# Input and forget gate projection of a two-layer trunk: eight weight columns stationary and 512 tokens streamed, in place of token blocks stationary and eight columns streamed

## The chip, the cores and the metric

The kernel runs on one core of one Trainium2 chip. The metric is the device time of one execution in microseconds (us). Three runs of the kernel before took 2545.02, 2545.56 and 2546.22 us; their median, 2545.56 us, is the time it is compared by. Engines are called PE (TensorE), PEld (TensorE's weight loads), DVE (VectorE), ACT (ScalarE), POOL (GpSimd) and SP (SyncE, which issues the DMAs).

## What is computed

Two layers run over 512 tokens of width 1024. Each layer is a half-step feed-forward block, a token mixer and a second half-step feed-forward block, each followed by a layer norm. The mixer is fed by one projection, cut here to what matters:

```
proj = x @ w_in + b_in
(aq, ak, av, mq, mk, mv, mo, mi, mf, cx, cb, cc, gates) = jnp.split(proj, _split_points(), axis=-1)
...
h = mlstm_chunkwise(mq..., mk..., mv..., mi, mf)      # mi, mf: 4 columns each, one per head
...
fc = chunk3(jax.nn.log_sigmoid(f_pre.astype(f32)))    # in mlstm_chunkwise; ic is i_pre itself
b = jnp.cumsum(ft, axis=-1)
```

The change is about `mi` and `mf`, the input and forget gates of the four mLSTM heads: 8 of the 7432 columns of `w_in`.

## The kernel before

The stream `x` lies transposed in on-chip memory, as 8 blocks (`k`) of 128 features by 512 tokens. Every large product is made of three matmuls in fp32r, a reduced format that PE takes in one pass: high part of the weights by high part of the stream, low by high, and high by low (lines 1341, 1342 and 1345). ACT makes the high parts by a copy that rounds (`wh`, `xh`), DVE the low ones by a subtraction (`wl`, `xl`).

Weights come in slabs of up to 1024 by 256, two slots in turn. For each slab SP loads `raw`, ACT writes `wh`, DVE writes `wl`, and PE runs the slab's matmuls, 128 stationary weight columns against 512 streamed tokens each. A slab can have a "middle job", work that PE does when half of its features are through, and an "end job" behind it. Nothing plans the order: on each engine it is that of the code in `mixer`, slab by slab (s = 0 to 39), and semaphores join the engines.

The gates do not go through slabs. The 8 columns are loaded into `wif` as they are (line 481). Behind slab 0, `gate_products` (line 1424) makes 32 matmuls in full fp32, 4 token blocks by 8 feature blocks: 128 by 128 of `x` is stationary and the 8 columns of `wif` are streamed (line 1430). The result has the tokens on the partitions, 8 columns for each token block. In s = 0 DVE adds the bias (line 1036), and DVE and ACT work out the logarithm of the sigmoid by turns (lines 1036 to 1042 and 671 to 675). In slab 2 the middle job turns the result by two transposes (lines 1443 and 1444), and scans follow.

While slab 0 runs, the layer norm ends: ACT writes `xh` and the final `x` block by block (lines 588 and 582), DVE writes `xl` (line 966). `stat_sums` has matmuls whose result is not used, in `keep_clock`, between its small ones (line 1372).

Of the kernel before, what the change touches and what calls it, by code (L numbers as in the profile page):

```python
# [73 lines left out]
def build(nc, xT, positions, w_in, w_branch, w_out, gu1, down1, gu2, down2, par_in, const_in, outT):  # L74
    ctx = ExitStack()
    with ctx:
# [83 lines left out]
        rst = place("rst", [P, 4])  # L160
        mrow = place("mrow", [1, 96])
        wif = place("wif", [P, KD, 8])
        lut = place("lut", [P, 1])

        tok = place("tok", [P, 5, NB])
# [14 lines left out]

        positions_in = tmp("positions_in", 8, [P, SEQ], I32)
        turns = tmp("turns", 8, [P, SEQ])
        angle = tmp("angle", 10, [P, SEQ])
        rf, ri, rb, ra, rloc, rg, rm, rz = (tmp(f"row{i}", 0.5 * i, [16, P]) for i in range(8))

# [67 lines left out]

        raw_in = [[Signal(f"raw_in{s}{h}", 16 * (S_LAYER // 2 + 1)) for h in range(2)] for s in range(2)]
        wif_in = Signal("wif_in", 16)
        start_in = Signal("start_in", 0)
        x_in = [Signal(f"x_in{k}", 0) for k in range(4)]
        pos_in = Signal("pos_in", 16)
# [47 lines left out]
        f_exp = Signal("f_exp", 1)  # L306
        f_one = Signal("f_one", 1)
        f_ln = Signal("f_ln", 1)
        gates_tok = Signal("gates_tok", 1)
        gate_in = Signal("gate_in", 1)  # L310
        rows_ps = Signal("rows_ps", 1)
# [52 lines left out]
        def f32(a):  # L364
            return a.bitcast(F32)
# [154 lines left out]
        def _(act):  # L520
# [146 lines left out]
            def memory_gates(layer, s):  # L667

                if s == 0:
                    act.wait_ge(gate_in.sem, gate_in.val(layer, 1))  # L670
                    act.activation(gs[:, :], gf[:, :], ACT.Abs).then_inc(*o.up(f_abs))
                    o.settle()
                    act.activation(gs[:, :], gs[:, :], ACT.Exp, scale=-1.0).then_inc(*o.up(f_exp))
                    act.wait_ge(f_one.sem, f_one.val(layer, 1))
                    act.activation(gs[:, :], gs[:, :], ACT.Ln).then_inc(*o.up(f_ln))
                if s == 4:
                    act.wait_ge(decay_row.sem, decay_row.val(layer, 1))
                    act.activation(mrow[0:1, 80:96], mrow[0:1, 64:80], ACT.Exp).then_inc(*o.up())
                    act.wait_ge(g_rows.sem, g_rows.val(layer, 1))

                    act.activation(rf[:, :], rg[:, :], ACT.Exp, bias=rz[:, 0:1], scale=-1.0).then_inc(*o.up())
                    act.activation(ri[:, :], rm[:, :], ACT.Exp, scale=-1.0).then_inc(*o.up())
                    act.activation(rb[:, :], ra[:, :], ACT.Exp, bias=rz[:, 1:2]).then_inc(*o.up(exp_rows))
# [41 lines left out]
                act.activation(yMh[:, h, :], ytmp[:, :], ACT.Copy).then_inc(*o.up(ym_hi))  # L725

            def mixer(layer):
                for s in range(S_MIX):
                    n = S_FFN + s
                    if s == 0:  # L730
                        split_half(layer, n + 1, 1)
                    else:
                        split(layer, n + 1)
                    if 7 <= s < 15:
                        attn_out(layer, s - 7)
                    if s >= 18 and s < 30:
                        h, r = divmod(s - 18, 3)
                        if r == 0:
                            mem1(layer, h)
                        if r == 1:  # L740
                            mem3(layer, h)
                        if r == 2:
                            mem4(layer, h)
                    if s < 18:
                        evacuate(layer, s)
                    elif s < 36:
                        t, r = divmod(s - 18, 3)
                        if r < 2:
                            act.wait_ge(slab_done.sem, slab_done.val(layer, n + 1))
                            for m in range(2):  # L750
                                b = B_G + 8 * BRANCH_ORDER[t // 2] + 4 * (t % 2) + 2 * r + m
                                if t > 0:

                                    act.wait_ge(prod.sem, prod.val(layer, 4 * (t - 1) + 2 * r + m + 1))
                                act.activation(gt[:, 2 * r + m, :], pm[2 * r + m][:, :], ACT.Sigmoid,
                                               bias=par[:, b:b + 1]).then_inc(*o.up(sig_ready))
                        elif t >= 4:
                            for m in range(4):
                                k = 4 * (t - 4) + m
                                act.wait_ge(merged.sem, merged.val(layer, k + 1))  # L760
                                act.activation(mh[k // 4][:, k % 4, :], x[:, k, :], ACT.Copy).then_inc(*o.up(mg_hi))
                    if s in (0, 4):
                        memory_gates(layer, s)
                    if 6 <= s < 14:
                        attn_pT(layer, s - 6)
                    if 5 <= s < 13:
                        attn_exp(layer, s - 5)
                    if s in (15, 16):
                        for c in (2 * (s - 15), 2 * (s - 15) + 1):
                            act.wait_ge(yc_f.sem, yc_f.val(layer, c + 1))  # L770
                            act.activation(yCh[:, c, :], convtmp[:, :], ACT.Copy).then_inc(*o.up(yc_hi))
                    if s == 23:

                        act.wait_ge(slab_done.sem, slab_done.val(layer, n + 1))
                        for c in range(4):
                            act.activation(yAh[:, c, :], yA[:, c, :], ACT.Copy).then_inc(*o.up(ya_hi))
                    if s >= 18 and s < 30 and (s - 18) % 3 == 0:
                        mem2(layer, (s - 18) // 3)
                    if s == 37:
                        centre_copy(layer, 1)  # L780
                        squares(layer, 1, 0)
                        squares(layer, 1, 1)
                    if s in (37, 38):
                        squares(layer, 1, 2 * (s - 36))
                        squares(layer, 1, 2 * (s - 36) + 1)
                norm_tail(layer, 1, n + 2)
# [66 lines left out]
        def _(dve):  # L853
# [173 lines left out]
                o.settle()  # L1027

            def memory_gates(layer, s):
                if s == 0:  # L1030

                    dve.wait_ge(gate_ps.sem, gate_ps.val(layer, 1))
                    g = sd[:, 3, 0:32].rearrange("p (n g) -> p n g", g=8)
                    for dst, c in ((gi, 0), (gf, 4)):
                        bias = par[:, PAR_IF + c:PAR_IF + c + 4].unsqueeze(1).broadcast_to([P, NB, 4])
                        ins = V.tensor_tensor(dst[:, :].rearrange("p (n h) -> p n h", h=4), g[:, :, c:c + 4], bias, ALU.add)
                    ins.then_inc(*o.up(gate_in))

                    dve.wait_ge(f_exp.sem, f_exp.val(layer, 1))
                    V.tensor_scalar(gs[:, :], gs[:, :], 1.0, None, ALU.add).then_inc(*o.up(f_one))  # L1040
                    dve.wait_ge(f_ln.sem, f_ln.val(layer, 1))
                    V.scalar_tensor_tensor(out=gf[:, :], in0=gf[:, :], scalar=0.0, in1=gs[:, :],
                                           op0=ALU.min, op1=ALU.subtract).then_inc(*o.up(gates_tok))
# [193 lines left out]
                dve.wait_ge(proj.sem, proj.val(layer, proj_count(s)))  # L1237

            def mixer(layer):
                for s in range(S_MIX):  # L1240
                    n = S_FFN + s
                    if s == 0:
# [2 lines left out]
                        split(layer, n + 1)  # L1245
                    h, r = divmod(s - 18, 3)

                    if s in (2, 3, 4, 5):
                        memory_gates(layer, s)
                    if 18 <= s < 30:  # L1250
                        (mem1, mem3, mem4)[r](layer, h)

                    if s == 0:
                        memory_gates(layer, s)
                        dve.wait_ge(table_ready.sem, table_ready.val(layer, 1))
                    if s == 1:
                        rope(layer, 0, q[:, 0, :], 0)
# [51 lines left out]
        def _(pe):  # L1309
# [113 lines left out]

            def gate_products(layer):

                pe.wait_ge(wif_in.sem, wif_in.val(layer, 16))
                pe.wait_ge(norm_ready.sem, norm_ready.val(layer, KD))
                for n in range(NB):
                    for k in range(KD):
                        ins = T.matmul(sd[:, 3, 8 * n:8 * n + 8], x[:, k, P * n:P * n + P], wif[:, k, :],  # L1430
                                       start=k == 0, stop=k == KD - 1)
                ins.then_inc(gate_ps.sem, 1)

            def rotate(layer, r, t, bank, s):
# [3 lines left out]
                T.matmul(sd[:, bank, :], const[:, K_ROT:K_ROT + P], t, start=True, stop=True).then_inc(rot_ps.sem, 1)  # L1438

            def middle_job(layer, s):  # L1440
                if s == 2:
                    pe.wait_ge(gates_tok.sem, gates_tok.val(layer, 1))
                    T.transpose(sd[0:16, 2, 0:128], gf[:, :], ident)
                    T.transpose(sd[0:16, 2, 128:256], gi[:, :], ident).then_inc(rows_ps.sem, 1)
# [253 lines left out]
```

## Time and profile before

| | |
|---|---|
| median of three runs | 2545.56 us |
| the profiled execution, first to last instruction (span) | 2544.7 us |
| PE busy | 2515.7 us, 99% of the span |
| PEld busy | 2053.7 us, 81% |
| DVE busy | 1131.2 us, 44% |
| ACT busy | 973.2 us, 38% |
| POOL busy | 217.8 us, 9% |
| mean granted TensorE clock | 0.993 of full |
| main matmuls, each of the three kinds | 2336 on `xh` or `xl`, 704 on the hidden layer, and 320 more |

The profile gives no time of its own for that execution beside the span. Each matmul's recorded duration holds its way through the array, so that rows overlap (0.39 us long, but starting 0.23 us apart); what a stretch of matmuls costs is read from the distance of their starts. The fp32 matmuls of the gates stand in the trace as two records each.

### The profile page before, as it was taken

How to read it: one execution, taken by the hardware profiler on the slowest of the kernel's cores; microseconds unless marked ns; L12 is line 12 of the kernel's file. 1: busy time of each engine (PE TensorE's matmuls, PEld its weight loads, DVE VectorE, ACT ScalarE, POOL GpSimd, SP SyncE). 2: the span in 40 equal slices, each digit the busy share in tenths (PEclk: the TensorE clock that was granted, in tenths of full speed). 3: DMA queues.
4: the chain of work that ended last, by engine and by line, in shares of the span. 5: the costliest groups of instructions: out<-in, count | busy, mean ns of one | idle time of the engine just before them, and what ended most of it. 6: DMA issues, size and time to landing. Idle time of an engine off the chain costs nothing.

```text
span 2544.7 us, 31255 instructions
## 1 busy us (share of the span) xinstructions
PE 2515.7 (99%) x11378; PEld 2053.7 (81%) x11378; DVE 1131.2 (44%) x1584; ACT 973.2 (38%) x1334; POOL 217.8 (9%) x136
## 2 busy tenths in 40 slices
PE   8999999999999999999999999999999999999997
PEld 7888877778888778888788888787788887888886
DVE  3333344455555653333433333544455547433335
ACT  4443233344343354432344432424344433544323
POOL 0002120000000310001200021200000003000012
PEclk9999999999999999999999999989999999999999
DMA  5233232222222222322233323222222232332232
GB/s 166 90 98 99 92 88 75 77 73 83 83 83 83 96 81 89 97 95 92 95 100 99 97 92 101 55 92 67 83 83 83 68 98 83 99 99 89 90 107 79
DMA packets 229324, 229.05 MB, mean 90 GB/s; under 512 B 9440, under 2 KB 220640, under 8 KB 229216
## 3 DMA queue, kind: packets, MB, share of 16 engines
q1 hardware_dynamic: 229216, 227.66, 28.1%
q8 instruction: 62, 1.02, 0.2%
q14 instruction: 46, 0.38, 0.0%
HBM read 225.53 MB, written 2.10 MB: 89 GB/s over the span
## 4 chain that ended last, share of the span: by engine, by line
PE 95%; issue 2%; DVE 2%; POOL 1%; ACT 0%; DMA 0%; DVEq 0%; POOLq 0%; SPq 0%
PE main L1341 29%; PE main L1345 29%; PE main L1342 29%; PE side L1555 1%; PE side L1430 1%; DVE x L972 1%; DVE xl L966 1%; POOL ln_Q L838 1%; PE side L1377 1%; PE side L1507 1%; PE side L1541 0%; PE side L1392 0%; PE main L1372 0%; PE side L1565 0%; POOL ln_S L837 0%
## 5 line engine op out<-in xcount | busy, mean ns | idle before, releaser
L1341 PE MATMUL main<-xh,wh 128*128 128x512 f32 x2336 | 923.2, 395 | 8.7 <-ACT xh L550 7.3
L1345 PE MATMUL main<-xl,wh 128*128 128x512 f32 x2336 | 915.2, 392 | 2.1 <-DVE xl L966 1.2
L1342 PE MATMUL main<-xh,wl 128*128 128x512 f32 x2336 | 912.5, 391 | 0.0
L864 DVE TENSOR_TENSOR wl<-raw,wh 128x1024 fp32r<-128x1024 f32 (+1 forms) x443 | 538.9, 1250 | 626.6 <-ACT wh L541 619.8
L541 ACT ACTIVATE wh<-raw 128x1024 fp32r<-128x1024 f32 (+1 forms) x443 | 431.2, 1013 | 544.7 <-PE main L1345 537.1
L1341 PEld LDWEIGHTS main<-xh,wh 128*128 128x128 f32 x2336 | 440.4, 189 | 110.5 <-issue 12.2
L1345 PEld LDWEIGHTS main<-xl,wh 128*128 128x128 f32 x2336 | 440.0, 188 | 106.6 <-DVE xl L966 13.3
L1342 PEld LDWEIGHTS main<-xh,wl 128*128 128x128 f32 x2336 | 440.4, 189 | 91.3 <-issue 1.4
L1341 PE MATMUL main<-hh,wh 128*128 128x512 f32 x704 | 273.9, 389 | 0.0
L1342 PE MATMUL main<-hh,wl 128*128 128x512 f32 x704 | 273.9, 389 | 0.0
L1345 PE MATMUL main<-hl,wh 128*128 128x512 f32 x704 | 273.9, 389 | 0.0
L987 DVE SCALAR_TENSOR_TENSOR hp<-main,sil 128x512 f32<-128x512 f32 x88 | 56.7, 686 | 322.0 <-PE main L1345 322.0
L606 ACT ACTIVATE hh<-hp 128x512 f32 x88 | 54.4, 636 | 317.8 <-DVE hp L987 317.8
L1345 PEld LDWEIGHTS main<-hl,wh 128*128 128x128 f32 x704 | 132.2, 188 | 27.7
L1342 PEld LDWEIGHTS main<-hh,wl 128*128 128x128 f32 x704 | 132.2, 188 | 27.6
L1341 PEld LDWEIGHTS main<-hh,wh 128*128 128x128 f32 x704 | 132.2, 188 | 27.1
L831 POOL TENSOR_TENSOR ln_Z<-x 128x512 fp32r<-128x512 f32 x6 | 13.2, 2196 | 1555.1 <-DVE x L889 942.9
L842 POOL TENSOR_TENSOR x<-x,ln_M 128x512 f32<-128x512 f32 x42 | 68.8, 1672 | 122.8 <-ACT ln_M L576 122.8
L992 DVE TENSOR_TENSOR hl<-hp,hh 128x512 f32 x88 | 59.6, 719 | 15.0 <-ACT hh L606 15.0
L562 ACT ACTIVATE ln_sq<-x 128x512 f32<-128x512 f32 x48 | 28.8, 626 | 92.5 <-DVE x L908 90.9
L541 ACT ACT_TABLE_LOAD x45 | 57.7, 1283 | 3.8 <-issue 2.2
L602 ACT ACT_TABLE_LOAD x44 | 56.5, 1283 | 0.8
(253 smaller groups left out, 2005.0 us busy)
## 6 DMA issues: line engine op xcount, KB each, us to landing
raw<-gu SPq DMA_DIRECT2D x180, 512.0 KB, 4.4
raw<-w_in SPq DMA_DIRECT2D x104, 512.0 KB, 4.5
raw<-down SPq DMA_DIRECT2D x80, 512.0 KB, 3.7
raw<-w_branch SPq DMA_DIRECT2D x24, 512.0 KB, 4.4
raw<-w_out SPq DMA_DIRECT2D x16, 512.0 KB, 4.4
raw<-w_in SPq DMA_DIRECT2D x24, 256.0 KB, 3.2
raw<-down SPq DMA_DIRECT2D x16, 256.0 KB, 3.8
x<-xT SPq DMA_DIRECT2D x4, 512.0 KB, 6.7
```

The costliest lines, as they stand in the source:

```text
L541: ins = act.activation(put(wh[slot]), get(raw[slot]), ACT.Copy)
L562: act.activation(ln_sq[m % 2][:, :], x[:, m, :], ACT.Square).then_inc(*o.up(sq_ready))
L602: act.activation(sil[0][:, :], pm[0][:, :], ACT.Silu).then_inc(*o.up(silu_ready))
L606: act.activation(hh[:, bass.ds(i * 2 + m, 1), :], hp[m][:, :].unsqueeze(1), ACT.Copy).then_inc(*o.up(hid_h))
L838: nc.gpsimd.tensor_tensor(Q, first[1], ln_sq[m % 2][:, :], ALU.add).then_inc(*o.up(part_sums))
L842: nc.gpsimd.tensor_tensor(x[:, m, :], x[:, m, :], ln_M[:, :], ALU.subtract).then_inc(*o.up(cen_ready))
L864: ins = V.tensor_tensor(put(wl[slot]), get(raw[slot]), f32(put(wh[slot])), ALU.subtract)
L987: V.scalar_tensor_tensor(out=hp[m][:, :], in0=pm[2 + m][:, :], scalar=0.5, in1=sil[m][:, :], op0=ALU.mult, op1=ALU.mult).then_inc(*o.up(hi ...
L992: V.tensor_tensor(hl[:, c, :], hp[m][:, :].unsqueeze(1), f32(hh[:, c, :]), ALU.subtract).then_inc(*o.up(hid_l))
L1341: T.matmul(out, hi, a, start=starts and k == 0, stop=False)
L1342: T.matmul(out, lo, a, start=False, stop=False)
L1345: ins = T.matmul(out, hi, b, start=False, stop=stops and k == kk - 1)
```

## The change

The 8 weight columns get a high and a low part of their own: `wifs`, 16 columns for each feature block, written once per layer by one ACT copy and one DVE subtraction at the start of the mixer. `gate_products` becomes 24 fp32r matmuls: for each of the 8 feature blocks the high and low columns are stationary against `xh`, and the high ones against `xl`, with all 512 tokens streamed. The result is 8 rows by 512 tokens in the same PSUM bank.

Since what follows wants tokens on the partitions, ACT copies the 8 rows to `grow` in s = 0, and a new middle job in slab 1 turns them by four transposes into another bank. What DVE and ACT do with the result (bias, logarithm of the sigmoid) moves from s = 0 to s = 1. The middle job of slab 2 stays.

```diff
+        wifs = place("wifs", [P, KD, 16], F32R)
...
+        grow = tmp("grow", 8, [8, SEQ])
...
             def memory_gates(layer, s):
 
                 if s == 0:
+                    act.wait_ge(gate_ps.sem, gate_ps.val(layer, 1))
+                    act.activation(grow[:, :], sd[0:8, 3, :], ACT.Copy).then_inc(*o.up(gate_row))
+                if s == 1:
                     act.wait_ge(gate_in.sem, gate_in.val(layer, 1))
                     act.activation(gs[:, :], gf[:, :], ACT.Abs).then_inc(*o.up(f_abs))
...
             def mixer(layer):
+                act.wait_ge(wif_in.sem, wif_in.val(layer, 16))
+                act.activation(wifs[:, :, 0:8], wif[:, :, :], ACT.Copy).then_inc(*o.up(wif_hi))
...
+                    if s == 1:
+                        memory_gates(layer, s)
                     if s < 18:
                         evacuate(layer, s)
...
             def memory_gates(layer, s):
-                if s == 0:
-
-                    dve.wait_ge(gate_ps.sem, gate_ps.val(layer, 1))
-                    g = sd[:, 3, 0:32].rearrange("p (n g) -> p n g", g=8)
+                if s == 1:
+
+                    dve.wait_ge(gate_tok.sem, gate_tok.val(layer, 1))
+                    g = sd[:, 2, 0:32].rearrange("p (n g) -> p n g", g=8)
...
             def mixer(layer):
+                dve.wait_ge(wif_hi.sem, wif_hi.val(layer, 1))
+                V.tensor_tensor(wifs[:, :, 8:16], wif[:, :, :], f32(wifs[:, :, 0:8]), ALU.subtract).then_inc(*o.up(wif_lo))
...
             def gate_products(layer):
 
-                pe.wait_ge(wif_in.sem, wif_in.val(layer, 16))
-                pe.wait_ge(norm_ready.sem, norm_ready.val(layer, KD))
-                for n in range(NB):
-                    for k in range(KD):
-                        ins = T.matmul(sd[:, 3, 8 * n:8 * n + 8], x[:, k, P * n:P * n + P], wif[:, k, :],
-                                       start=k == 0, stop=k == KD - 1)
+                pe.wait_ge(wif_lo.sem, wif_lo.val(layer, 1))
+                rows = sd[0:8, 3, :]
+                for k in range(KD):
+                    T.matmul(rows, wifs[:, k, 0:8], xh[:, k, :], start=k == 0, stop=False)
+                    T.matmul(rows, wifs[:, k, 8:16], xh[:, k, :], start=False, stop=False)
+                    ins = T.matmul(rows, wifs[:, k, 0:8], xl[:, k, :], start=False, stop=k == KD - 1)
                 ins.then_inc(gate_ps.sem, 1)
...
             def middle_job(layer, s):
+                if s == 1:
+                    pe.wait_ge(gate_row.sem, gate_row.val(layer, 1))
+                    apart(pe)
+                    for n in range(NB):
+                        ins = T.transpose(sd[:, 2, 8 * n:8 * n + 8], grow[:, P * n:P * n + P], ident[0:8, 0:8])
+                    ins.then_inc(gate_tok.sem, 1)
```

On PE, between the last matmul of slab 0 and the first of slab 1, stood this before (`main` is a PSUM bank of a slab, `side` the bank of the gates):

```order
L1345 MATMUL main1<-xl_51,wh0_54 128x512
L1426 ISA
L1430 MATMUL side<-wif_115,x_49 128x8 [waits norm_ready,wif_in]
L1430 MATMUL side<-wif_115,x_49 128x8 x31
L1330 REGISTER_ALU
L1341 MATMUL main2<-xh_50,wh1_55 128x512 [waits w_lo]
```

The same place now begins so; the last three of these rows come eight times, and behind them stands the first matmul of slab 1:

```order
L1359 MATMUL main1<-xl_51,wh0_54 128x512
L1440 REGISTER_ALU
L1443 MATMUL side<-xh_50,wifs_116 8x512 [waits wif_lo]
L1444 MATMUL side<-xh_50,wifs_116 8x512
L1445 MATMUL side<-xl_51,wifs_116 8x512
```

So 32 matmuls with an 8-wide stream became 24 with a 512-wide one, and the wait for `x` became one for the low part of the gate columns.

In the middle of slab 1, PE now has the new job, where two main matmuls followed each other directly before:

```order
L1356 MATMUL main3<-xh_50,wl1_57 128x512
L1359 MATMUL main3<-xl_51,wh1_55 128x512
L1344 REGISTER_ALU
L1459 MATMUL side<-const_93,grow_131 128x8 [waits w_lo,gate_row]
L1459 MATMUL side<-const_93,grow_131 128x8 x3
L1355 MATMUL main2<-xh_50,wh1_55 128x512
```

Four transposes are added there, behind a wait for ACT's copy of the rows.

On ACT, from the last block of the norm on, the queue before was this (`wh_55` is slab 1's second half, `wh_54` slab 2's):

```order
L582 ACTIVATE x<-x,par 128x512 [waits x_ready]
L541 ACTIVATE wh_55<-raw_53 128x4x128 [waits raw_in11]
L541 ACTIVATE wh_55<-raw_53 128x4x128
L641 REGISTER_ALU
L665 ACTIVATE q<-main,par 128x512 [waits slab_done]
L665 ACTIVATE q<-main,par 128x512
L671 ACTIVATE gs<-gf 128x16 [waits gate_in]
L673 ACT_TABLE_LOAD
L673 ACTIVATE gs<-gs 128x16 [waits f_abs]
L675 ACT_TABLE_LOAD
L675 ACTIVATE gs<-gs 128x16 [waits f_one]
L539 REGISTER_ALU [waits slab_done]
```

Now it begins so:

```order
L588 ACTIVATE x<-x,par 128x512 [waits x_ready]
L737 ISA
L738 ACTIVATE wifs<-wif 128x8x8 [waits wif_in]
L547 ACTIVATE wh_55<-raw_53 128x4x128 [waits raw_in11]
L547 ACTIVATE wh_55<-raw_53 128x4x128
L647 REGISTER_ALU
L671 ACTIVATE q<-main,par 128x512 [waits slab_done]
L671 ACTIVATE q<-main,par 128x512
L676 REGISTER_ALU
L677 ACTIVATE grow<-side 8x512 [waits gate_ps]
L545 REGISTER_ALU [waits slab_done]
L547 ACTIVATE wh_54<-raw_52 128x512 [waits raw_in00]
```

The copy of the gate columns stands ahead of slab 1's second half, the copy of the rows takes the place of the three activations and two table loads, and these come behind slab 2's `wh`.

## Rows read from the trace of the kernel before

**Rows 1.** The page: chain that ended last, shares of the span by line.

```profile
PE main L1341 29%; PE main L1345 29%; PE main L1342 29%; PE side L1555 1%; PE side L1430 1%; DVE x L972 1%; DVE xl L966 1%; POOL ln_Q L838 1%; PE side L1377 1%; PE side L1507 1%; PE side L1541 0%; PE side L1392 0%; PE main L1372 0%; PE side L1565 0%; POOL ln_S L837 0%
```

**Rows 2.** Line 1430's instructions: count, duration ns min/median/max, first and last start us.

```profile
L1430 PE MATMUL side<-wif,x x128: 170/361/362, 390.8 to 1662.0; 128*128 128x8 f32 x128
```

**Rows 3.** Stretches, all engines: length, each engine's busy us and instructions, PEclk, DMA, GB/s.

```profile
390.75:400.84 10.09, 10.09 (x65) 10.09 (x64) 1.29 (x2) 1.41 (x3) 0.00 (x0) 0.69 0.20 54
1651.25:1662.23 10.98, 10.98 (x65) 10.98 (x64) 1.29 (x2) 1.41 (x3) 0.00 (x0) 0.63 0.19 49
390.75:413.64 22.89, 22.89 (x114) 20.53 (x112) 3.19 (x8) 5.67 (x10) 0.00 (x0) 0.78 0.25 70
1651.25:1675.79 24.54, 24.54 (x114) 21.93 (x112) 3.19 (x8) 5.66 (x10) 0.00 (x0) 0.72 0.22 65
400.84:404.79 3.95, 3.95 (x10) 3.12 (x11) 0.60 (x4) 3.42 (x6) 0.00 (x0) 0.51 0.00 0
```

**Rows 4.** Stretches of 1 us, line 1430 alone: length, PE, PEld, PEclk, DMA, GB/s.

```profile
393.00:394.00 1.00, 1.00 (x11) 1.00 (x11) 1.00 0.30 46
394.00:395.00 1.00, 1.00 (x9) 1.00 (x8) 0.75 1.06 312
...
1653.00:1654.00 1.00, 1.00 (x11) 1.00 (x11) 1.00 0.01 1
1654.00:1655.00 1.00, 1.00 (x7) 1.00 (x7) 0.51 0.86 191
```

**Rows 5.** PE in order of time, slab 1: start us, us, instruction.

```profile
401.41 0.63 PE L1342 MATMUL main<-xh,wl 128*128 128x512 f32 x1
...
404.40 0.55 PE L1345 MATMUL main<-xl,wh 128*128 128x512 f32 x1
...
405.02 0.39 PE L1342 MATMUL main<-xh,wl 128*128 128x512 f32 x1
...
413.41 0.39 PE L1345 MATMUL main<-xl,wh 128*128 128x512 f32 x1
413.64 1.88 PE L1438 MATMUL side<-q,const 128*128 128x512 f32 x4
...
415.58 0.40 PE L1342 MATMUL main<-xh,wl 128*128 128x512 f32 x1
```

**Rows 6.** PE in order of time, middle jobs of slabs 2 and 5.

```profile
417.90 0.39 PE L1345 MATMUL main<-xl,wh 128*128 128x512 f32 x1
...
418.57 0.40 PE L1342 MATMUL main<-xh,wl 128*128 128x512 f32 x1
...
446.52 0.39 PE L1345 MATMUL main<-xl,wh 128*128 128x512 f32 x1
446.83 0.42 PE L1459 MATMUL side<-const,row 16*128 16x16 f32 x4
...
447.74 0.39 PE L1342 MATMUL main<-xh,wl 128*128 128x512 f32 x1
```

**Rows 7.** DVE in order of time around the gates.

```profile
387.48 1.62 DVE L966 SCALAR_TENSOR_TENSOR xl<-x,par,xh 128x512 fp32r<-128x512 f32 x2
...
401.03 0.17 DVE L1036 TENSOR_TENSOR gi<-side,par 128x16 f32<-128x16 f32 x1 [8.80 <-PE side L1430]
...
404.62 0.17 DVE L1042 SCALAR_TENSOR_TENSOR gf<-gf,gs 128x16 f32<-128x16 f32 x1 [1.35 <-ACT gs L675]
...
420.18 0.27 DVE L1047 COPY row<-side 16x128 f32<-16x128 f32 x1
```

**Rows 8.** ACT in order of time: start of the mixer, and two copies from PSUM later.

```profile
389.13 0.72 ACT L582 ACTIVATE x<-x,par 128x512 f32<-128x512 f32 x1 [0.15 <-DVE xl L966]
389.76 1.14 ACT L541 ACTIVATE wh<-raw 128x512 fp32r<-128x512 f32 x2
...
509.51 0.60 ACT L697 ACTIVATE pT<-side 128x512 f32<-128x512 f32 x1
...
518.11 0.36 ACT L702 ACTIVATE yA<-side 128x256 f32<-128x256 f32 x1
```

**Rows 9.** The DMA into `wif`, two issues (first 336.1): us to landing.

```profile
DMA to landing us min/median/max: 3.4/3.5/3.6
```

More of the change, by code:

```diff
@@ L255, in build @@
         wif_in = Signal("wif_in", 16)
+        wif_hi = Signal("wif_hi", 1)
+        wif_lo = Signal("wif_lo", 1)
         start_in = Signal("start_in", 0)
@@ L308, in build @@
         f_ln = Signal("f_ln", 1)
+        gate_row = Signal("gate_row", 1)
+        gate_tok = Signal("gate_tok", 1)
         gates_tok = Signal("gates_tok", 1)
@@ L1246, in mixer @@
                     h, r = divmod(s - 18, 3)
-                    if s in (2, 3, 4, 5):
+                    if 1 <= s < 6:
                         memory_gates(layer, s)
@@ L1253, in mixer @@
                     if s == 0:
-                        memory_gates(layer, s)
                         dve.wait_ge(table_ready.sem, table_ready.val(layer, 1))
```

## The prediction

> **What bounds the kernel now.** I read the busy shares, then the chain that ended last, then PE in order of time around the changed line. PE is busy for 99% of the span, and the chain is nearly all PE: the three kinds of main matmuls make 87% of it, and line 1430, the gate products, 1% [rows 1]. DVE (44%) and ACT (38%) wait for PE. So time on PE is time of the kernel, microsecond for microsecond, as long as nobody else becomes late; and line 1430 has a place in the chain.
>
> The gate products are 128 records, 64 in each layer, two for each of the 32 matmuls [rows 2]. Their block lasts 10.09 us in the first layer and 10.98 us in the second [rows 3]. The reader is to see two things in these rows. PE counts as busy through the whole block, yet only 8 columns are streamed by each matmul: the time is that of loading 128 by 128 of `x` each time. And the granted clock is 0.69 and 0.63 over the block: it is 1.00 at first (2.4 GHz), with 11 records in a microsecond, and then 0.50 (1.2 GHz), with 6 or 7. The fall lies at about 394.5 in the first layer (the mean of that microsecond is 0.75) and at about 1654.0 in the second [rows 4]: 3.75 and 2.75 us after the block's start. What PE did before the fall was loading weights with almost no streaming. The clock stays at half into slab 1: 0.51 from 400.84 to 404.79 [rows 3].
>
> So the block costs more than its own length. The full price is read over block and slab 1 together, up to the first rotation (line 1438). At full clock the main matmuls start (413.41 - 405.02) / 37 = 0.2268 us apart [rows 5] (37 steps lie between the two), so slab 1's 48 take 10.88 us. The stretches are 22.89 and 24.54 us long [rows 3]. What is left for the gates is 12.01 us in layer 0 and 13.66 us in layer 1, **25.67 us in all**: 21.07 of blocks, and 4.60 of slab 1's matmuls at the lower clock.
>
> **The change part by part.**
>
> *The products.* 32 matmuls go and 24 come, each streaming 512 columns like a main matmul. The trace has none with 8 stationary columns, so I bound it. From above the nearest row is the main matmul: 128 columns loaded, 0.2268 us. I see no row in which fewer columns cost more. From below it can't be less than 512 columns at 2.4 GHz, 0.2133 us, if loading 8 columns hides wholly. I take 0.2268, since the stream is the same: 24 x 0.2268 = **5.44 us a layer** (5.12 at the lower end). That holds if the clock stays up, which I take as the likeliest: slabs of such streams run at 1.00 wherever I looked, and what preceded the fall was the lack of streaming. No row shows whether a stream through 8 of 128 columns counts the same; the first rival takes the other case. With a dense stream, slab 1 starts at full clock too.
>
> By the Trainium skill, "TensorE: Matmul & The Clock Gate", Part 2 (Back-to-back issue gap), isolated matmuls at full clock start about 2.5 ns further apart than their streaming takes; the main matmuls here need 13 ns above it. By that rule the block would be an estimated 5.2 us a layer and the total half a microsecond lower than mine; the row of this case decides for me. The same page, Part 1, has the clock follow how busy PE has been; by the records here PE was busy all through the block in which the clock fell [rows 3], so a busy record is no promise that the clock stays.
>
> *The four transposes in slab 1.* Each loads a piece of 8 by 128 and streams 8 columns. Nearest above: in slab 5 four such of 16 by 128 and one small fp32 matmul stand between two main ones; from 446.52 to 447.74 there are 1.22 us where two steps would be 0.45, so 0.77 us for all five [rows 6]. Nearest below: the two transposes in slab 2, 417.90 to 418.57, 0.67 - 0.45 = 0.22 us. Four of them without the small matmul I put at **0.5 us a layer**.
>
> *Waits on PE at the block.* Out goes the wait for `x`; in comes one for the low part of the gate columns. `wif` lands 3.5 us after its issue at 336.1, long before [rows 9]. ACT does its copy where `wh` began before, at 389.76 [rows 8]. The copy has 64 elements a partition; 256 take 0.36 us [rows 8], so at most that, and I take 0.25. DVE is free from 389.10 (387.48 + 1.62) and needs about 0.2 (16 elements 0.17, 128 elements 0.27) [rows 7]. The low part is ready at about 390.3 and at the latest at 390.5. PE needs it at 390.75, less 0.2 for the load ahead. I take **0**; 0.3 us a layer if the copies are slower. Behind this wait all of PE would queue.
>
> *What the two copies hold up.* Slab 1's second half (`wh`, `wl`) comes 0.25 to 0.5 us later, at about 392.7; PE wants it at 390.75 + 5.44 + 5.44 = 401.6. Covered by 9 us.
>
> *ACT's copy of the rows.* The block ends at 396.2. A 512-element copy from PSUM takes 0.60 us [rows 8]; with 0.2 us of signal it is there at 397.0. The middle of slab 1 is at 401.6. Covered by 4.6 us. Behind it on ACT is slab 2's `wh`, which started at 404.49 before and now starts at 397. It gets earlier, and SP's load that waits for slab 2's low part with it. Slabs 0 and 1 give the other engines nothing new to wait for there.
>
> *The logarithm of the sigmoid, one slab later.* The transposes end at about 402.1, DVE starts at 402.3, and the chain of DVE and ACT with its two table loads lasts 404.79 - 401.03 = 3.76 us [rows 7]: ready at 406.1. Slab 1 ends at 396.19 + 10.88 + 0.5 = 407.6, so ACT is back for its evacuation and DVE for the rotations. The consumer, the middle job of slab 2, comes 1.3 us of rotations and 12 matmuls (2.7 us) later, at 411.6. Slack 5.5 us. From there all runs as before, only earlier.
>
> *The sum.* Out 25.67, in 2 x (5.44 + 0.5) = 11.88, so **-13.8 us**. The profiled span is 2544.7 us, 0.9 below the median of the runs; the profile gives nothing between the two, and a stretch in the middle does not touch what lies around. 2545.56 - 13.8 = **2531.8 us**. The case's own range goes from 2530 (products at 0.2133: -0.6; transposes at 0.22: -0.6; a little more) to 2534 (transposes at 0.77: +0.5; waits of 0.3 twice: +0.6; a stray microsecond elsewhere).
>
> **Rivals.**
>
> *A. The clock falls in the new block as well.* For it: PE was "busy" in the old block too, and here 120 of 128 columns of the array stand still. Against it: the stream is now dense, and every slab with dense streams shows 1.00. Price: let it fall after the same 3.75 and 2.75 us. At the lower clock the starts are (404.40 - 401.41) / 7 = 0.427 us apart [rows 5]. In layer 0, 3.75 us bring 16.5 matmuls and the other 7.5 take 3.2: 6.95. In layer 1, 12.1 and 11.9: 7.83. The tails in slab 1 stay, 12.01 - 10.09 = 1.92 and 13.66 - 10.98 = 2.68. With the transposes 9.4 and 11.0 a layer: 5.3 saved, **2540.3 us**.
>
> *B. A narrow fp32r matmul runs in four passes* (the slower side). Place: the 24 matmuls themselves. The only full fp32 matmuls with 512 columns streamed, the two of line 1438, hold PE from 413.64 to 415.58, 1.94 - 0.23 = 1.71 us, 0.86 each [rows 5]. If a stationary operand of 8 columns lost the one-pass path, the block would be 24 x 0.86 = 20.6 us: with the transposes 21.1 against 12.01 and 13.66, +16.5, **2562 us**. It decides from 0.51 us a matmul, (12.84 - 0.5) / 24. For it: no row shows fp32r with under 128 columns. Against it: the type is what sets the passes in all rows here, not the width.
>
> *C. The change is hidden or given back.* The gate chain's new place costs a wait (at slab 2's middle job, or at the low part) that eats most of the gain, or a later stage is released at its old time by a transfer. For it: two new waits on PE. Against it: slacks of 4.6 and 5.5 us, and no main matmul of this part waits for DMA. It would take 9 us or more to come within 0.2%: about **2542 us**.
>
> **How the numbers follow.** Forecast 0.78, A 0.14, B 0.04, C 0.04. No change that this measurement can tell means within 0.2%, 5.1 us. The forecast is faster by 0.54%; A by 0.21%, so half of it counts as faster and half as same; C as same; B as slower. Faster 0.85, same 0.11, slower 0.04. The range is to hold 0.8: the forecast's own 2530 to 2534, and up to A's value, of which it takes in the milder half (a fall in one layer alone gives 2536): **2529.5 to 2540.5**.
>
> **What would show it.** Right: a block of 24 matmuls 5.1 to 5.5 us long in both layers, granted clock 1.00 in it and in all of slab 1; slab 1 with a gap near 0.5 us at its middle; no wait of PE for DVE's low part of the gate columns; DVE's first rotation 5.9 to 6.2 us earlier than before in layer 0, and its counterpart in layer 1 some 13.8 us earlier. Wrong: a granted clock under 1 between the block's start and slab 1's end (A); starts 0.4 us or more apart at full clock (B); idle PE ahead of the block or of a middle job (C).

## The result and the profile after

The changed kernel took 2532.85 us (median of 4 runs, 2532.12 to 2533.04), the kernel before 2545.86 us beside it (2545.02 to 2546.22): a ratio of 0.9949, 95% interval [0.9935, 0.9963]. The gain is 13.0 us; forecast were 2531.8 us and a gain of 13.8. One run of the last experiment took 6508.64 us; it is left out of that experiment's numbers, and no trace shows why.

The page of the changed kernel has a span of 2531.2 us, 13.5 less than before, and line 1430's successors no longer stand among the lines that its chain lists (line 1430 had 1%; they are still in the chain, with 0.23 us a matmul). Where [rows 3] had stretches with a clock of 0.63 to 0.78, the same stretches now read so (length, then busy us and instructions of PE, PEld, DVE, ACT and POOL, granted clock, DMA share, GB/s):

```profile
390.88:396.42 5.54, 5.54 (x25) 2.21 (x24) 1.29 (x2) 1.46 (x3) 0.00 (x0) 1.00 0.36 95
390.88:407.89 17.01, 17.01 (x77) 11.46 (x76) 3.20 (x8) 6.30 (x11) 0.00 (x0) 1.00 0.32 92
1645.40:1650.95 5.55, 5.55 (x26) 2.21 (x24) 1.29 (x2) 1.47 (x3) 0.00 (x0) 1.00 0.35 94
1645.40:1662.41 17.01, 17.01 (x77) 11.46 (x76) 3.20 (x8) 6.31 (x11) 0.00 (x0) 1.00 0.32 92
```

The block is 5.54 us long, and the clock is 1.00 in it and in slab 1. Block and slab 1 up to the first rotation take 17.01 us in both layers, where they took 22.89 and 24.54 [rows 3]. Less 10.88 us for slab 1's own matmuls, the gates cost 6.13 us a layer, 12.26 in all, in place of 25.67: 13.41 of the 13.5 us by which the span shrank.

PE in order of time (start, duration, instruction) shows the block's end, and the middle of slab 1 with the transposes:

```profile
395.73 0.40 PE L1443 MATMUL side<-xh,wifs 128*8 128x512 f32 x1
395.96 0.40 PE L1444 MATMUL side<-xh,wifs 128*8 128x512 f32 x1
396.20 0.39 PE L1445 MATMUL side<-xl,wifs 128*8 128x512 f32 x1
396.42 0.39 PE L1355 MATMUL main<-xh,wh 128*128 128x512 f32 x1
396.65 0.39 PE L1356 MATMUL main<-xh,wl 128*128 128x512 f32 x1
...
401.64 0.39 PE L1359 MATMUL main<-xl,wh 128*128 128x512 f32 x1
401.95 0.41 PE L1459 MATMUL side<-const,grow 8*128 8x8 f32 x4
402.29 0.50 PE L1355 MATMUL main<-xh,wh 128*128 128x512 f32 x1
402.63 0.40 PE L1356 MATMUL main<-xh,wl 128*128 128x512 f32 x1
```

After the narrow matmuls the main ones start 0.23 us apart at once; [rows 5] had 0.43 there. The helpers, ACT's two copies, DVE's low part and the end of the gate chain, in order of time:

```profile
389.90 0.24 ACT L738 ACTIVATE wifs<-wif 128x64 fp32r<-128x64 f32 x1
...
396.62 0.59 ACT L677 ACTIVATE grow<-side 8x512 f32<-8x512 f32 x1 [4.28 <-PE side L1445]
```

```profile
390.18 0.23 DVE L1254 TENSOR_TENSOR wifs<-wif,wifs 128x64 fp32r<-128x64 f32 x1 [0.94 <-ACT wifs L738]
...
402.40 0.17 DVE L1049 TENSOR_TENSOR gi<-side,par 128x16 f32<-128x16 f32 x1 [3.35 <-PE side L1459]
...
405.99 0.18 DVE L1055 SCALAR_TENSOR_TENSOR gf<-gf,gs 128x16 f32<-128x16 f32 x1 [1.35 <-ACT gs L684]
```

The low part is there at 390.41. The block's first weights are loaded from 390.65 and its first matmul starts at 390.88, and no wait of PE stands ahead of either. The chain ends at 406.17, and slab 2's middle job needs it at 412.38.

### The profile page after: what moved, and what is told of

Its sections match the earlier page's. It is cut to its first block, busy times and chain, and to the rows that moved or that the text cites. A ratio compares the mean times of both kernels' runs of the same rounds, so it can differ in the third digit from the quotient of the medians.

```text
span 2531.2 us, 31119 instructions
## 1 busy us (share of the span) xinstructions
PE 2502.2 (99%) x11306; PEld 2034.1 (80%) x11306; DVE 1131.7 (45%) x1586; ACT 974.5 (38%) x1338; POOL 218.0 (9%) x136
## 4 chain that ended last, share of the span: by engine, by line
PE 95%; DVE 2%; issue 2%; POOL 1%; ACT 0%; DMA 0%; DVEq 0%; POOLq 0%; SPq 0%
PE main L1355 29%; PE main L1359 29%; PE main L1356 29%; PE side L1575 1%; DVE x L985 1%; DVE xl L979 1%; POOL ln_Q L851 1%; PE side L1391 1%; PE side L1527 1%; PE side L1561 0%; PE side L1406 0%; PE main L1386 0%; PE side L1585 0%; POOL ln_S L850 0%; PE side L1495 0%
## 5 line engine op out<-in xcount | busy, mean ns | idle before, releaser
L1359 PEld LDWEIGHTS main<-xl,wh 128*128 128x128 f32 x2336 | 439.0, 188 | 105.9 <-DVE xl L979 13.6
```

What stands on the lines that cost most here:

```text
L1359: ins = T.matmul(out, hi, b, start=False, stop=stops and k == kk - 1)
```

## The experiments

For each kernel the price of the gates is read as above: from the block's start to the first rotation of q, less 10.88 us. "Before" is the kernel before, run on the same chip. The price and the clock are read from one traced execution of each kernel, the medians from all runs.

| kernel | median us | before | gates us, layer 0 / 1 | clock there |
|---|---|---|---|---|
| changed | 2532.85 | 2545.86 | 6.13 / 6.13 | 1.00 |
| e1 dense between | 2551.56 | 2545.66 | 16.84 / 15.19 | 0.69 / 0.74 |
| e2 halves | 2541.68 | 2545.66 | 10.43 / 10.40 | 0.84 |
| e3 orientation alone, fp32 | 2535.55 | 2545.66 | 7.77 / 7.77 | 1.00 |
| e4 sixteen | 2530.09 | 2545.66 | 4.93 / 4.93 | 1.00 |
| e5 quarters | 2534.73 | 2545.78 | 7.39 / 7.38 | 1.00 |
| e6 one feature block | 2522.67 | 2545.78 | 0.96 / 0.95 | 1.00 |
| e7 double | 2543.43 | 2545.78 | 11.68 / 11.69 | 1.00 |
| e8 sixteen transposed | 2529.20 | 2545.78 | 4.30 / 4.35 | 1.00 |

**e6: the whole old price, measured by leaving most of it out.** The gates are made from one feature block; the products of the other seven are left out.

```diff
                 for n in range(NB):
-                    for k in range(KD):
-                        ins = T.matmul(sd[:, 3, 8 * n:8 * n + 8], x[:, k, P * n:P * n + P], wif[:, k, :],
-                                       start=k == 0, stop=k == KD - 1)
+                    ins = T.matmul(sd[:, 3, 8 * n:8 * n + 8], x[:, 0, P * n:P * n + P], wif[:, 0, :],
+                                   start=True, stop=True)
```

> The kernel before with 4 gate matmuls a layer in place of 32: the products of feature block 0 alone, the other seven feature blocks are left out of the gates. Measures the whole price of the gate products directly. If 12.0 and 13.7 us (blocks and slow tails read in the trace) are right: 28/32 of the records and the tails go, 8 records of 0.09 us and about 0.2 us of change remain, 0.9 us a layer, so 25.7 - 1.9 = 23.8 us less, 2521.9 us. If the price were the blocks' length alone (21.1 us): 2526.5 us.

The median fell by 23.1 us and the span by 23.7 (from 2544.7 of the kernel before to 2521.0); expected was 23.8. The ratio is 0.9909 [0.9894, 0.9925]. The block's length alone would have given 19.2. So the reading over block and slab 1 was right: the slow matmuls of slab 1 were part of the price, and in the trace they are gone with the products (clock 1.00).

**e1: dense matmuls between the old products.**

```diff
                         ins = T.matmul(sd[:, 3, 8 * n:8 * n + 8], x[:, k, P * n:P * n + P], wif[:, k, :],
                                        start=k == 0, stop=k == KD - 1)
+                        if k % 4 == 3 and (n, k) != (NB - 1, KD - 1):
+                            T.matmul(pm[2][:, :], xh[:, 0, 0:P], xh[:, 1, :], start=True, stop=True)
```

> The kernel before, with seven dense fp32r matmuls (128 stationary columns, 512 streamed, result unused) put between the 32 gate matmuls of each layer, one behind every fourth. Work is only added: 7 x 0.227 = 1.6 us a layer. Theory (half of the old price was the clock): the granted clock stays at 1.00 through block and slab 1, the 64 records take 0.091 us each, 5.8 us, so the gates cost 7.4 to 7.8 us a layer in place of 12.0 and 13.7, and the kernel takes about 2535.7 us, faster than before by some 10 us. Rival (the old price is that of 64 loads of 128 by 128, the clock a by-product): it gets slower by 3.2 us or more, 2549 us.

My theory fell in this form: 5.9 us slower, ratio 1.0022 [1.0013, 1.0031], as the rival said (3.2 us or more). But the trace does not bear out the rival's mechanism. Stretches of 1 us, PE alone (length, busy, granted clock, DMA, GB/s):

```profile
391.00:392.00 1.00, 1.00 (x10) 1.00 0.00 0
392.00:393.00 1.00, 1.00 (x10) 0.77 0.33 50
393.00:394.00 1.00, 1.00 (x5) 0.50 1.07 318
...
408.00:409.00 1.00, 1.00 (x4) 0.50 0.00 0
409.00:410.00 1.00, 1.00 (x5) 0.70 0.00 0
410.00:411.00 1.00, 1.00 (x6) 1.00 0.40 53
```

In layer 0, shown here, the clock fell all the same, about 3 us into the block, and came back only 6 us into slab 1. In order of time, two rounds of the same work at the two clocks:

```profile
389.68 0.95 PE L1430 MATMUL side<-wif,x 128*128 128x8 f32 x8
390.49 0.49 PE L1433 MATMUL main<-xh 128*128 128x512 f32 x1
390.81 0.95 PE L1430 MATMUL side<-wif,x 128*128 128x8 f32 x8
...
395.66 1.71 PE L1430 MATMUL side<-wif,x 128*128 128x8 f32 x8
397.22 0.77 PE L1433 MATMUL main<-xh 128*128 128x512 f32 x1
397.79 1.71 PE L1430 MATMUL side<-wif,x 128*128 128x8 f32 x8
```

A round takes 390.81 - 389.68 = 1.13 us before the fall and 397.79 - 395.66 = 2.13 after it. With one dense matmul in each round the clock did not hold. By the starts of main matmuls such a matmul is worth 0.23 us, a fifth of the round; but eight records at 0.091 us are only 0.73 of the 1.13, so that it cost 0.40 with the changes from one kind to the other, and "7 x 0.227 = 1.6 us a layer" was too low.

Whether the filler also kept the clock down for longer, the two layers answer differently. At half clock PE spent about 17.1 us in layer 0 (392.5 to 409.6), where the kernel before had 10.2 (394.5 to 404.7), but 13.6 in layer 1 (1658.9 to 1672.5), where it had 13.7 (1654.0 to 1667.7). So the price rose by 4.8 us in one layer and by 1.5 in the other. The run left open whether more dense work would hold the clock; e2 and e5 were for that, in another form.

**e2 and e5: the old products in pieces.** The order is changed, not the products; bias and logarithm of the sigmoid stand in slab 1, as in the changed kernel. e2's core:

```diff
             def middle_job(layer, s):
                 if s == 1:
-                    ... (four transposes)
+                    gate_products(layer, (2, 3))
...
             def end_job(layer, s):
                 if s == 0:
-                    gate_products(layer)
+                    gate_products(layer, (0, 1))
```

> The old fp32 products, in two halves: token blocks 0 and 1 behind slab 0, 2 and 3 in the middle of slab 1; the bias and the logarithm of the sigmoid in slab 1 as in the changed kernel; no split gate columns, no transposes. Theory: each half is 2.9 us at full clock and dense work stands between, so the clock stays at 1.00 or nearly (in layer 1 it fell after 2.75 us, so a short fall is possible there); gates 6.0 to 6.5 us a layer, 2532.5 to 2534 us, as fast as the changed kernel. Rival (the gain comes from the new orientation): the old products cost their 10 to 11 us wherever they stand, 2541 to 2546 us.

e2 took 2541.68 us, ratio 0.9987 [0.9978, 0.9996]. The number is the rival's (2541 to 2546), but not for the rival's reason. The stretches in layer 0, PE alone, are first half of the products, first half of slab 1, second half of the products, second half of slab 1:

```profile
390.21:393.69 3.48, 3.48 (x33) 1.00 0.15 29
393.69:400.85 7.16, 7.16 (x27) 0.76 0.66 206
400.85:404.62 3.77, 3.77 (x34) 0.92 0.02 4
404.62:411.52 6.90, 6.90 (x25) 0.80 0.00 0
```

The products themselves ran at full clock nearly throughout: 3.48 + 3.77 = 7.25 us, where the one block had 10.09. Yet the clock fell as each half ended, and the slow microseconds were main matmuls: 7.16 and 6.90 us for halves of 5.44. Slab 1 so lost 1.72 + 1.46 = 3.18 us to the clock, where the kernel before lost 22.89 - 10.09 - 10.88 = 1.92. Of what the blocks gave back, nearly half went there.

A rival that I had not named can be settled here. The falls of the kernel before come with a burst of DMA traffic (312 and 191 GB/s in those microseconds [rows 4]), and so does e1's (318 the microsecond after). But the second fall of e2 has next to none around it, PE alone in stretches of 1 us:

```profile
403.00:404.00 1.00, 1.00 (x11) 1.00 0.00 0
404.00:405.00 1.00, 1.00 (x6) 0.52 0.08 16
405.00:406.00 1.00, 1.00 (x3) 0.50 0.00 0
```

And the changed kernel keeps 1.00 through a burst of 256 GB/s in the middle of its block, from 394 to 395. So the DMA traffic is not the cause. Quarters of the products, in e5:

```diff
-                    gate_products(layer, (2, 3))
+                    gate_products(layer, (2,))
...
-                        slab(layer, n, pair, xhk, xlk, middle=mid, **(stream_wait(layer, 1) if s == 0 else {}))
+                        quarter = lambda k: gate_products(layer, (k // 2,)) if k in (2, 6) else None
+                        slab(layer, n, pair, xhk, xlk, middle=mid,
+                             **(stream_wait(layer, 1) if s == 0 else {"before_k": quarter}))
```

> As e2_halves, in four parts: token block 0 behind slab 0, then one token block each ahead of features 2, 4 and 6 of slab 1, so that 1.45 us of gate products alternate with 12 main matmuls (2.7 us). In e1 seven dense matmuls between the gate products did not keep the clock, and in e2 it fell after each half, by the time the gate products had ended. Theory (the clock answers to how much streaming there has been over the last few microseconds, so each stretch of gate products must be short beside dense work): the clock stays at 1.00, the gates cost 5.8 us of records and four changes of kind at 0.2 to 0.3 us, 6.8 us a layer, 2534.5 us. Rival (any gate product in slab 1 pulls the clock down): as e2 or worse, 2541 to 2546 us.

2534.73 us against an expected 2534.5; ratio 0.9957 [0.9944, 0.9971]. The page's stretches of both layers, PE alone:

```profile
389.97:408.24 18.27, 18.27 (x114) 1.00 0.29 88
1645.81:1664.07 18.26, 18.26 (x113) 1.00 0.30 88
```

The same 32 fp32 matmuls, with the same 64 loads of 128 columns, now cost 7.4 us a layer in place of 12.0 and 13.7. What changed on PE is that each 1.7 us of them stands beside 2.9 us of main matmuls, and the clock does not fall. That is 11.0 of the change's 13 us, got without new operands, copies or transposes. The products' 64 records alone would take 5.8 us a layer at full clock (11 in a microsecond [rows 4]); the other 1.6 us are four changes from one kind of matmul to the other.

**e3: the orientation alone.**

```diff
-                pe.wait_ge(wif_lo.sem, wif_lo.val(layer, 1))
+                pe.wait_ge(wif_in.sem, wif_in.val(layer, 16))
+                pe.wait_ge(norm_ready.sem, norm_ready.val(layer, KD))
                 rows = sd[0:8, 3, :]
                 for k in range(KD):
-                    ... (three fp32r matmuls)
+                    ins = T.matmul(rows, wif[:, k, :], x[:, k, :], start=k == 0, stop=k == KD - 1)
```

> The changed kernel with the orientation alone: 8 full fp32 matmuls, the 8 columns of wif as loaded stationary and x streamed; no high and low parts, transposes as changed. Theory: four passes, 0.86 us each as line 1438 has them, 6.9 us a layer at clock 1.00 in place of 5.54, so +2.7 us against the changed kernel, 2535.5 us. If fp32 with 8 stationary columns is slower than with 128, it is later by 8 times the difference a layer. If the clock falls in it, 2 to 4 us more.

2535.55 us, as expected; ratio 0.9959 [0.9946, 0.9973]. In order of time:

```profile
389.42 0.39 PE L1355 MATMUL main<-xl,wh 128*128 128x512 f32 x1
389.74 7.03 PE L1440 MATMUL side<-x,wif 128*8 128x512 f32 x16
396.70 0.50 PE L1351 MATMUL main<-xh,wh 128*128 128x512 f32 x1
```

Eight full fp32 matmuls take 6.96 us, 0.87 each, the same as with 128 columns stationary (0.86, [rows 5]). The split into high and low parts saves 7.77 - 6.13 = 1.64 us a layer on top. Beside e5 this says more: where the clock stays up, the same fp32 products cost 7.39 us in the old orientation, in quarters, and 7.77 in the new one with its transposes. So in full fp32 the new orientation is not the cheaper one by itself; what it gives is the clock, and a form in which the one-pass matmuls pay. fp32r products in the old orientation were not tried.

**e7: the narrow stream, twice as long.**

```diff
-                for k in range(KD):
+                for again in range(2):
+                    for k in range(KD):
```

> The changed kernel with its 24 narrow matmuls done twice (same result), a block of 11.1 us with 8 of 128 columns stationary and a dense stream. Theory (streaming keeps the clock, however few columns are stationary): granted clock 1.00 through block and slab 1, 24 x 0.231 = 5.54 us a layer more, +11.1 us against the changed kernel, 2544 us. Rival A of the prediction, seen only in a longer block: the clock falls some 3 to 7 us into it, and the kernel takes 2550 us or more.

2543.43 us, 10.6 above the changed kernel; 11.1 were expected, and the gates' price did rise by 5.55 us a layer. In this trace the block starts 0.45 us earlier than in the changed kernel's, so the missing half microsecond lies ahead of it. The clock (all engines' stretches; the number behind POOL's) is 1.00 through the block and through the block with slab 1:

```profile
390.43:401.53 11.10, 11.10 (x50) 1.00 0.18 47
390.43:412.99 22.56, 22.56 (x101) 1.00 0.24 70
```

11.1 us with 8 of 128 columns stationary, longer than the old block, did not lower the clock. Rival A is out.

**e4 and e8: sixteen columns at once.**

```diff
-                    T.matmul(rows, wifs[:, k, 0:8], xh[:, k, :], start=k == 0, stop=False)
-                    T.matmul(rows, wifs[:, k, 8:16], xh[:, k, :], start=False, stop=False)
-                    ins = T.matmul(rows, wifs[:, k, 0:8], xl[:, k, :], start=False, stop=k == KD - 1)
+                    T.matmul(rows, wifs[:, k, :], xh[:, k, :], start=k == 0, stop=False)
+                    ins = T.matmul(rows, wifs[:, k, :], xl[:, k, :], start=False, stop=k == KD - 1)
```

> The changed kernel with the high and low columns stationary together, 16 columns: 16 fp32r matmuls a layer in place of 24, result 16 rows; the four transposes become four fp32 matmuls that add the high and the low row while they turn them. Theory (the streaming of 512 columns is the price, whatever is stationary): 8 x 0.231 = 1.85 us a layer less, about 0.15 more for the turning, so -3.4 us against the changed kernel, 2529.4 us. Rival (16 columns cost more than 8): no gain, 2532.9 us.

2530.09 us; ratio 0.9937 [0.9924, 0.9951]. The block shrank from 5.54 to 3.71 us as expected, but turning by fp32 matmuls costs two records each:

```profile
399.21 0.39 PE L1360 MATMUL main<-xl,wh 128*128 128x512 f32 x1
399.53 1.05 PE L1459 MATMUL side<-const,grow 16*128 16x8 f32 x8
400.51 0.50 PE L1356 MATMUL main<-xh,wh 128*128 128x512 f32 x1
```

That is 1.2 us a layer in place of 0.6; the difference was put at 0.15, so the kernel is 0.7 us slower than expected. e8 turns by plain transposes and lets DVE add:

```diff
-                        ins = T.transpose(sd[:, 2, 8 * n:8 * n + 8], grow[:, P * n:P * n + P], ident[0:8, 0:8])
+                        ins = T.transpose(sd[:, 2, 16 * n:16 * n + 16], grow[:, P * n:P * n + P], ident[0:16, 0:16])
...
+                    for dst, c in ((gi, 8), (gf, 12)):
+                        d3 = dst[:, :].rearrange("p (n h) -> p n h", h=4)
+                        ins = V.tensor_tensor(d3, d3, g[:, :, c:c + 4], ALU.add)
```

> As e4_sixteen, but the 16 rows are turned by four plain transposes, and DVE adds the low columns to the high ones with two more small operations. In e4 the block was 3.71 us a layer in place of 5.54, but the four fp32 matmuls that turned and added took 1.2 us in place of 0.6. Theory: transposes of 16 rows cost as those of 8, 0.6 us; DVE's 0.4 us more lies in the slack of the gate chain; gates 4.3 us a layer, 1.8 us less than in the changed kernel, 2529.2 us.

2529.20 us, as expected; ratio 0.9936 [0.9922, 0.9949]. It lies below the changed kernel's 2532.85 us, but that was measured apart from it; the last pair was to compare the two on one chip.

> The changed kernel again, on the same chip as the next one, so that the two can be compared: 2532.9 us.

> The kernel of e8 again beside the changed kernel. If its gain is real (gates 4.3 us a layer in place of 6.1), its runs lie 3.4 to 3.7 us below those of the changed kernel on this chip; if the 2529.2 us of e8 came from another chip, less.

The changed kernel took 2532.82 us (5 runs, 2532.04 to 2533.51) and this one 2528.62 (5 runs, 2528.28 to 2529.62), with ratios to the kernel before of 0.9949 [0.9936, 0.9962] and 0.9933 [0.9920, 0.9946]. The difference is 4.2 us, 0.5 to 0.8 more than expected; by the two traces the gates are 1.83 us a layer cheaper, 3.7 in all, and the rest is not explained. The intervals of the two ratios overlap, but the runs of the two kernels do not, and two executions of the same kernel lie up to 1.5 us apart here.

## Why the prediction was right

- **What the old products cost.** 12.01 + 13.66 us with the slow tails. e6 took out all but 1.9 us of them and shortened the span by 23.7 us, as this sum says.
- **The new block.** Forecast 5.44 us a layer, measured 5.54: the narrow matmuls start 0.2308 us apart, the main ones 0.2268. My bounds for one matmul, 0.2133 to 0.2268, did not hold it: "I see no row in which fewer columns cost more" was no ground for an upper end. That is 0.2 us in all, and it put the block outside the 5.1 to 5.5 us that were to show the forecast right. By the Trainium skill's rule for isolated matmuls (2.5 ns above the streaming, "TensorE: Matmul & The Clock Gate", Part 2) it would have been less; measured in this stream are 17.5 ns above 0.2133, so the trace does not bear it out.
- **The clock.** It stayed at 1.00, the likeliest case. No row had settled this, as the prediction says; e7 does now, and shows that not even 11 us of such a stream would lower it. e1 and e2 show the other side: loads of 128 by 128 with 8 columns streamed lower it, with single dense matmuls among them (e1) and in stretches of 3.5 us (e2), though not in stretches of 1.7 us (e5). Busy time in the records says nothing of it, since PE was busy in all of them.
- **The transposes.** Forecast 0.5 us, measured 17.01 - 5.54 - 10.88 = 0.59: another 0.2 us in all.
- **The waits.** None on PE. The low part was ready 0.47 us before the block's start and 0.24 before its first weights were loaded, the smallest margin of all; the chain's slack was 6.2 us, 5.5 forecast. ACT's copy of the rows was done at 397.21, 4.7 us ahead of its use at 401.95. Rival C did not come.
- **Passes.** Rival B is out: a narrow fp32r matmul takes one pass, 0.23 us, and e3 has the four-pass price beside it, 0.87. (Line 1438's are not the only full fp32 matmuls with 512 columns streamed, as the prediction says; lines 1392 and 1472 have more. The price does not depend on it.)
- **The rotations.** DVE's first one began 414.69 - 408.95 = 5.74 us earlier in layer 0, and 1676.85 - 1663.47 = 13.38 us earlier in layer 1; forecast were 5.9 to 6.2 and some 13.8. Both fall short by the two small terms above, and the first also by a block that started 0.13 us later in this trace.
- **The sum.** -13.8 forecast, -13.4 by the stretches, -13.5 by the spans, -13.0 by the medians. The last half microsecond lies in which execution was profiled. The spans of the kernel before go with its mean clock: in the last pair's runs 2543.1 to 2543.4 us at 0.994, and 2543.6 to 2545.1 at 0.993; the profiled one had 2544.7 at 0.993. A run lies 1.8 us above its own span, not 0.9: I had set a long span against the median of other runs. So the 2532.85 us lie 1.05 above the forecast: 0.4 of it is the two small terms, 0.3 the kernel before, whose median was 2545.86 beside this run and not 2545.56, and the rest is this scatter.
- **What I had not weighed.** I priced the clock's part as 4.60 us of slow tails, though half of the block ran slow too. At full clock the block's 64 records would take about 5.8 us; so by this estimate 21.07 - 2 x 5.8 = 9.5 us of blocks were the clock's as well, 14 us with the tails, and e5 got 11.0 us back with the old products (3 us went to its changes of kind). The sum was not touched by this, but the reading of the change was: most of its gain is the clock, less is that of fewer or shorter matmuls. That the narrow operand is stationary matters because loads with little streaming become streams with little loading.

## What to carry to other kernels

When a small product costs more than it should on a busy TensorE, read the granted clock through it and through the dense work behind it: the slow microseconds behind it belong to its price. Stream the long side and keep the narrow one stationary; if that can't be done, break the product into short pieces between dense matmuls; here pieces of 1.7 us with 2.9 us of dense work behind each gave 11 of 13 us, and pieces of 3.5 us, half a slab apart, gave 4. Once the stream is what costs, put high and low columns into one stationary operand, and turn the result by transposes (0.6 us for four) rather than by fp32 matmuls (1.2).

## What the runs showed of the hardware

- Seven dense matmuls among 32 load-bound ones did not hold the clock. The time at half clock grew from 10.2 to 17.1 us in layer 0 and stayed as it was in layer 1 (13.7 and 13.6), and the kernel got 5.9 us slower. Here a filler this thin was worse than none.
- The clock can fall when the product that lowered it has already ended: in e2 its cost fell on main matmuls, 1.72 and 1.46 us a half in layer 0. It fell with heavy DMA traffic and with none.
- The runs of a kernel whose clock falls scatter more: 2548.71 to 2552.7 us in e1 and 2540.86 to 2544.29 in e2, where four of eleven lie at 2544.2 and seven at 2540.9 to 2541.8, against 2534.65 to 2534.95 in e5 and 2542.93 to 2544.05 in e7. The traced execution of e2 is one of the seven.
- Narrow fp32r matmuls, 8 or 16 columns, start 4 to 5 ns further apart than ones with 128. Their loads are shorter (0.088 us for 8 columns, 0.188 for 128). What makes the difference wasn't tried.
